# Product-key queries in one-pass products of split operands

## The chip, the cores and the metric

The kernel runs on one core of a Trainium2 chip. The metric is the device time of one execution in microseconds (us), the median of several executions. The engines are named as the profile names them: PE (TensorE matmuls), DVE (VectorE), ACT (ScalarE), POOL (GpSimd) and SP (SyncE, which issues most transfers).

## The reference, cut to what matters

One layer of a hybrid encoder trunk for 1024 prompt tokens and 64 sample tokens with 1024 channels. Its second half, which the change touches, is a retrieval of experts by product keys (PEER): for each token and each of 8 heads, a query with two halves of 128 channels, scores against 128 keys per half, the best 16 of each half, the best 16 of their sums, and then 16 experts out of 16384, each a row of a table `u` and a row of a table `v`.

```python
h = rmsnorm(x, norm2) * (1.0 + sc2) + sh2
x = x + g2 * peer(h, peer_wq, peer_keys, peer_u, peer_v)

def one_block(xb):                       # in peer, h in blocks of tokens
    q = (xb @ w_q).reshape(PEER_BLOCK, PEER_HEADS, 2, PEER_DQ // 2)
    s = jnp.einsum("nhcd,hckd->nhck", q, sub_keys).astype(jnp.float32)
    v1, i1 = lax.top_k(s[:, :, 0], PEER_TOPK)
    v2, i2 = lax.top_k(s[:, :, 1], PEER_TOPK)
    cand = (v1[..., :, None] + v2[..., None, :]).reshape(...)
    cidx = (i1[..., :, None] * PEER_NKEYS + i2[..., None, :]).reshape(...)
    top_s, pos = lax.top_k(cand, PEER_TOPK)
    eidx = jnp.take_along_axis(cidx, pos, axis=-1)
    gate = jax.nn.softmax(top_s, axis=-1)
    act = jax.nn.gelu(jnp.einsum("nd,nhkd->nhk", xb, u_tab[eidx]).astype(jnp.float32))
    coef = (gate * act).astype(xb.dtype)
    return jnp.einsum("nhk,nhkd->nd", coef, v_tab[eidx])
```

## The kernel before, in words

The five engines run programs of their own, written out by hand, and meet at semaphores. The order of each engine's program is the order of its work; nothing is planned at run time except a fixed assignment of PSUM banks (`plan`, `jobs`, `bank_for`) that says which engine empties which bank.

The first half of the layer ends with `mix` and the residual sum. DVE then normalizes the rows (`normed`, into `xn2`), PE transposes them (`turn("h2T", ...)`, 24 banks), and ACT and DVE turn each bank into columns of h2 by a scale and a bias (`modulated`, L329 and L332), taking alternate banks. h2 lies in `h2_buf` as float32, 8 blocks of 128 channels by 1088 tokens.

The head stage follows. For each of 8 heads PE runs six `query` groups (two halves c, three chunks of 384, 384 and 320 tokens), each of 8 float32 matmuls that accumulate over the 1024 channels (L904), and two `key_scores` groups of 9 matmuls (L919). The weights of a head, 128 x 2048, lie in one half of `wq_buf`, which SP loads two heads ahead; ACT copies the head's keys out of a block of all keys. Between every two query matmuls PE transposes half a tile of the u table (`turn_half`, four transposes of 128x128 into bank 6 or 7, L887), 14 tiles a head. ACT copies what PE made: a half tile back into one of 7 buffers (`table_half`, L1258), a query chunk (`q_move`, L1273), a group of scores (`s_moves`, L1286 and L1287, which waits until DVE has read the scores of the head before). SP stores each turned tile into `u_table` and loads the tile four later (`turn_table`). 128 tiles go this way; the rest is turned behind the last head.

DVE picks (`head_picks`): the top 16 of each half by maxima, index searches and replacements (L1868, L1873, L1875), the sums of the candidates (operations with two SBUF inputs), the top 16 of these sums, small integer operations, and a comparison with which it releases POOL (`positions_ready`). POOL decodes the indices of the head (`decode`, L584 to L601) while DVE goes on with the next one; DVE waits for the decode of the head before only ahead of its small operations. The softmax is shared: DVE subtracts the maximum, ACT takes the exponentials (`softmax_exp`, L1253 and L1254), and DVE sums them (L1951) and makes the gates. In ACT's program, the exponentials of head h-1 stand in the middle of head h, behind the copies of tile 10 and the last query chunk.

Behind the last head PE transposes the first 512 tokens of h2 back into rows (L952). Tokens from 512 on are needed later as a high part and a residual (`h_hi`, `h_lo`): ACT copies the high part, rounded, behind the last tile, and DVE subtracts (a rounded copy and the rest, which together hold the float32 value and let a product run as three products in one-pass format, `parts`). Then PE turns the picks, DVE and ACT make one-hots, PE the coefficients of the dense part, and POOL's gathers of table rows run beside the dense products until the end.

## Time and profile before

| what | before |
|---|---|
| three runs | 3021.05, 3023.61, 3029.80 us; median 3023.61 |
| profiled execution | 3024.45 us, span 3022.7 us, mean granted clock 0.97 |
| PE busy | 2822.1 us (93%) |
| PE weight loads | 2371.7 us (78%) |
| DVE busy | 2576.8 us (85%) |
| ACT busy | 911.7 us (30%) |
| POOL busy | 1579.1 us (52%) |

The busy times are sums over the whole span, and the stages differ. The page cuts the span in 40 slices of 75.6 us; the digits are tenths of busy time, and `PEclk` is the clock that TensorE was granted, in tenths of full speed. The head stage lies in slices 8 to 14.

```profile
PE   7999799999998577699999999999999999999996
PEld 3566358677776476699999999999999999999995
DVE  6481355369999999699999999999999999999998
ACT  3213230244444699312121121111211111112122
POOL 0000000025757000577777777777777777777772
PEclk9999899999999799899999999999999999999998
```

### The profile page before, as it was taken

To read this page: it belongs to the slowest core of one execution; us is meant where nothing else is said; L and a number is where in the kernel's file an instruction comes from. 1 tells how busy PE (TensorE), PEld (TensorE's weight loads), DVE (VectorE), ACT (ScalarE), POOL (GpSimd) and SP (SyncE) were. 2 spreads that over 40 slices of the span, in tenths; PEclk is the share of its full clock that TensorE was granted. 3 is DMA by queue.
4 is the path that set the end of the run, shared out by engine and by line. 5 is a ranking of instruction groups with operands and counts; after the bars stand their busy time and mean duration, and the time that the engine had idled before them with its cause. 6 is when DMAs were issued, how large, how long until landed. Compare 5 with 4: busy or idle time off the path is not lost.

```text
span 3022.7 us, 48458 instructions
## 1 busy us (share of the span) xinstructions
PE 2822.1 (93%) x16748; PEld 2371.7 (78%) x16748; DVE 2576.8 (85%) x5660; ACT 911.7 (30%) x1792; POOL 1579.1 (52%) x1211
## 2 busy tenths in 40 slices
PE   7999799999998577699999999999999999999996
PEld 3566358677776476699999999999999999999995
DVE  6481355369999999699999999999999999999998
ACT  3213230244444699312121121111211111112122
POOL 0000000025757000577777777777777777777772
PEclk9999899999999799899999999999999999999998
DMA  5012631499998566999999999999999999999996
GB/s 214 21 41 44 224 128 66 179 330 335 337 329 314 197 193 184 360 405 408 409 410 410 410 403 400 408 410 410 408 404 400 409 410 403 410 406 403 407 409 245
DMA packets 327375, 959.19 MB, mean 317 GB/s; under 512 B 38224, under 2 KB 119936, under 8 KB 313808
## 3 DMA queue, kind: packets, MB, share of 16 engines
q0 software_dynamic: 147456, 536.94, 44.8%
q1 hardware_dynamic: 167136, 412.46, 37.2%
q10 hardware_dynamic: 12688, 8.67, 1.0%
q8 instruction: 43, 0.70, 0.1%
q14 instruction: 52, 0.43, 0.0%
HBM read 840.97 MB, written 116.85 MB: 317 GB/s over the span
## 4 chain that ended last, share of the span: by engine, by line
PE 30%; DVE 26%; DMA 14%; issue 14%; POOL 11%; ACT 4%; DVEq 0%; ACTq 0%; SPq 0%; POOLq 0%
DMA ring<-in_vt,arena 12%; POOL ring L630 11%; PE ps L904 6%; DVE h_rows L2040 5%; DVE ring L2019 5%; PE ps L763 4%; PE ps L887 2%; PE ps L713 2%; PE ps L1010 2%; DVE u_lo L1479 2%; ACT arena L1342 2%; DVE y_rows L2040 2%; PE ps L861 2%; PE ps L870 2%; DVE arena L1479 2%
## 5 line engine op out<-in xcount | busy, mean ns | idle before, releaser
L630 POOL DMA_INDIRECT ring<-u_table,arena x512 | 690.3, 1348 | 375.4 <-PE ps L984 154.6
L630 POOL DMA_INDIRECT ring<-in_vt,arena x512 | 644.1, 1258 | 205.7 <-issue 134.8
L1010 PE MATMUL ps<-h_hi,u_hi 128*128 128x320 f32 (+1 forms) x2048 | 650.7, 318 | 35.1 <-DVE u_lo L1479 33.2
L2019 DVE SCALAR_TENSOR_TENSOR ring<-ring,h_rows 128x1024 f32<-128x1024 f32 x512 | 623.0, 1217 | 35.9 <-DMA ring<-u_table,arena 29.0
L1010 PE MATMUL ps<-h_lo,u_hi 128*128 128x320 f32 (+1 forms) x2048 | 607.4, 297 | 0.0
L1010 PE MATMUL ps<-h_hi,u_lo 128*128 128x320 f32 (+1 forms) x2048 | 607.3, 297 | 0.0
L1027 PE MATMUL ps<-w,v_rows 128*128 128x320 f32 (+1 forms) x2048 | 579.5, 405 | 0.0
L2040 DVE SCALAR_TENSOR_TENSOR h_rows<-ring,s5c,h_rows 128x1024 f32<-128x1024 f32 x381 | 489.7, 1285 | 41.9 <-DMA ring<-in_vt,arena 41.1
L1010 PEld LDWEIGHTS ps<-h_hi,u_hi 128*128 128x128 f32 x2048 | 389.5, 190 | 55.4 <-issue 25.3
L1027 PEld LDWEIGHTS ps<-w,v_rows 128*128 128x128 f32 x2048 | 358.3, 189 | 54.4
L1010 PEld LDWEIGHTS ps<-h_lo,u_hi 128*128 128x128 f32 x2048 | 389.5, 190 | 5.3
L1010 PEld LDWEIGHTS ps<-h_hi,u_lo 128*128 128x128 f32 x2048 | 389.2, 190 | 0.0
L1395 ACT ACTIVATE w<-ps 128x320 f32<-128x320 f32 (+1 forms) x256 | 104.7, 409 | 909.7 <-PE ps L1010 905.6
L1024 PE MATMUL ps<-w_hi,v_hi 128*128 128x320 f32 (+1 forms) x1024 | 366.0, 357 | 3.0 <-DVE y_sum L1479 3.0
L595 POOL TENSOR_TENSOR arena<-arena 128x2048 f32<-128x2048 f32 (+1 forms) x28 | 73.2, 2638 | 509.0 <-DVE arena L1479 508.5
L1479 DVE TENSOR_TENSOR arena<-arena 128x512 f32<-128x512 f32 (+17 forms) x229 | 187.0, 847 | 157.0 <-ACT arena L1175 62.9
L1024 PE MATMUL ps<-w_hi,v_lo 128*128 128x320 f32 (+1 forms) x1024 | 301.8, 295 | 0.0
L1024 PE MATMUL ps<-w_lo,v_hi 128*128 128x320 f32 (+1 forms) x1024 | 301.7, 295 | 0.0
L904 PE MATMUL ps<-h,wq 128*128 128x384 f32 (+1 forms) x768 | 266.9, 471 | 0.9 <-ACT h L329 0.9
L1024 PEld LDWEIGHTS ps<-w_hi,v_hi 128*128 128x128 f32 x1024 | 193.4, 189 | 24.6 <-DVE y_sum L1479 4.0
L1024 PEld LDWEIGHTS ps<-w_hi,v_lo 128*128 128x128 f32 x1024 | 193.4, 189 | 20.2
L984 PE MATMUL ps<-arena 128*128 128x128 f32 x1152 | 147.7, 285 | 54.8 <-DVE arena L2004 33.8
(279 smaller groups left out, 4337.4 us busy)
## 6 DMA issues: line engine op xcount, KB each, us to landing
u_turn<-in_ut SPq DMA_DIRECT2D x128, 512.0 KB, 5.3
u_table<-u_turn SPq DMA_DIRECT2D x128, 512.0 KB, 4.1
v_rows<-in_vt SPq DMA_DIRECT2D x64, 1024.0 KB, 11.0
u_raw<-in_ut SPq DMA_DIRECT2D x126, 512.0 KB, 6.7
coef_dram<-arena SPq DMA_DIRECT2D x8, 4096.0 KB, 15.9
c_raw<-coef_dram SPq DMA_DIRECT2D x64, 512.0 KB, 8.5
arena<-in_w_ada SPq DMA_DIRECT2D x24, 1024.0 KB, 7.5
arena<-in_xp SPq DMA_DIRECT2D x2, 4096.0 KB, 12.8
```

Source lines behind the costliest of these rows:

```text
L595: last = nc.gpsimd.tensor_tensor(v4, v4, itf[0:n, c, t0:t0 + nt, :].unsqueeze(2).to_broadcast(shp), ALU.mult)
L630: nc.gpsimd.indirect_dma_start(out=slot(n), out_offset=None, in_=table, in_offset=bass.IndirectOffsetOnAxis(ap=uvi[:, at:at + 1], axis=0)) ...
L763: last = mm(b[:, 0:width], w[:, k, P * m:P * m + P], h[:, k, P * k0:P * k0 + width], start=k == 0, stop=k == 7)
L904: last = mm(ps[q][:, 0:width], w[:, k, :], h2[:, k, P * k0:P * k0 + width], start=k == 0, stop=k == 7)
L984: last = mm(bank[:, j % 4, :], ar(PQ + 2048 * (g % 4) + P * j, P), ar(PQ + 2048 * (g % 4) + 1024 + P * j, P), start=True, stop=True)
L1010: last = mm(ps[b0 + j if first else j % 2][:, 0:width], w[a][:, k, :], ph[b][:, k, 64 * c0:64 * c0 + width], start=k == 0 and n == 0, stop ...
L1024: mm(out, v[r][:, P * d:P * d + P], w[r][:, 64 * c0:64 * c0 + width], start=begin and r % 2 == 0 and i == 0, stop=False, skip_group_check= ...
L1027: last = mm(out, v_row_buf(r)[:, 1024 + P * d:1024 + P * d + P], seg(w_in_buf, 1152 * r + ND + 64 * c0, width), start=False, stop=r % 2 == ...
L1395: av(seg(w_in_buf, o, width), ps[b0 + j if early and r < 2 else j % 2][:, 0:width], ACT.Gelu_apprx_tanh).then_inc(s("s_gelu"), 1)
L1479: return V.tensor_tensor(o, a, b, op)
L2019: V.scalar_tensor_tensor(out=row, in0=row, scalar=1.0, in1=h_rows[:, bass.ds(1024 * tile_of[0], 1024)], op0=ALU.mult, op1=ALU.mult, accum_ ...
L2040: V.scalar_tensor_tensor(out=y, in0=slot(at), scalar=acts[:, u, p:p + 1], in1=y, op0=ALU.mult, op1=ALU.add).then_inc(s("v_rows_done"), 1)
```

## The change

The queries are computed as the later dense products are: h2 is kept as a high part and a residual in the one-pass format (`s_hi`, `s_lo` for tokens 0 to 511, `h_hi`, `h_lo` for the others), the weights too, and each query group is three products per block of channels. The chunks are 512, 320 and 256 tokens. h2 is split before the first query: ACT or DVE computes each piece twice from its PSUM bank, once as float32 and once rounded, and DVE subtracts; the float32 buffer holds 512 tokens and is used twice. The last transposes, of 64 tokens, share one bank (17 banks for 24).

The weights of a head: ACT makes the high part (`wq_first`, two copies of 1024 columns a head, into one of two buffers), POOL the residual in the place of the weights (`wq_rest`, two subtractions, ahead of the decode of the head two earlier). PE's first query of each half waits for the residual. Keys come by two buffers, head by head, from SP.

The table has 6 buffers for 7 and 15 tiles a head for 14, 12 for 19 behind the last head. Head 0 has an order of its own on PE and ACT. The h2 rows are made by matmuls with a rounded identity from both parts. The split of h2 behind the last tile (ACT's copy and DVE's subtraction) is gone, and so are the waits for it.

The diff, cut to what the text speaks of:

```diff
-XN2, H2T = 0, 9216
-
-IALL, PICK, WQ, KEYS, QT, SB, WK = 17920, 21376, 27136, 31232, 33280, 35456, 37760
+XN2, HF, SHI, SLO, IDR = 33920, 43136, 9216, 13312, 51968
+
+IALL, PICK, WQ, KEYS, QT, SB, WK, WQH = 17408, 20864, 27136, 31232, 33280, 35456, (37760, 47232), (49792, 31232)
 CAND, CW2, D1, D0 = 38016, 40320, 42624, 44928
-TURN = (23296, 24320, 25344, 4608, 5632, 6656, 7680)
-NTURN, TPH = 7, 14
+TURN = (22784, 23808, 24832, 25856, 47744, 48768)
+NTURN, TPH = 6, 15
+QCH = ((0, 512), (512, 320), (832, 256))
+NSPLIT = 17
...
+            load(ar(WK[0], 256), A["keys"][:, 0:256], "wq_in0")
             load(seg(wq_buf, 0, 2048), A["wq"][0], "wq_in0")
             load(seg(wq_buf, 2048, 2048), A["wq"][1], "wq_in1")
             sp.wait_ge(bank_full, where["h2T", 7] + 1)
-            for r in range(3):
+            for r in range(4):
                 load(turn_buf[r][:, :], A["ut"][r], f"ut_in{r}")
-            stage_emptied(sp, "h2T")
-            load(turn_buf[3][:, :], A["ut"][3], "ut_in3")
+            sp.wait_ge(s("h_split"), NSPLIT)
+            load(ar(WK[1], 256), A["keys"][:, 256:512], "wq_in1")
...
-                    if not (first and r < 3):
-                        sp.wait_ge(s(f"table_out{b}"), 64 * i + 16 * ((r - 3) // NTURN) + 16)
+                    if not (first and r < NTURN - 4):
+                        sp.wait_ge(s(f"table_out{b}"), 80 * i + 16 * ((r + 4 - NTURN) // NTURN) + 16)
...
+                        load(ar(WK[h], 256), A["keys"][:, bass.ds(512 * i + (512 + 256 * h), 256)], f"wq_in{h}")
...
-            with pool.Fori(0, HEADS - 1) as h:
-                decode(h)
+            def wq_rest(h, hb):
+                for c in range(2):
+                    o = 2048 * hb + 1024 * c
+                    pool.wait_ge(s("wq_hi_ready"), 2 * h + c + 1)
+                    nc.gpsimd.tensor_tensor(wq_lo[:, o:o + 1024], seg(wq_buf, o, 1024),
+                                            wq_hi[hb][:, 1024 * c:1024 * c + 1024].bitcast(F32),
+                                            ALU.subtract).then_inc(s("wq_lo_ready"), 1)
+
+            wq_rest(0, 0)
+            wq_rest(1, 1)
+            with pool.Fori(0, HEADS // 2 - 1) as i:
+                for hb in range(2):
+                    wq_rest(2 * i + (hb + 2), hb)
+                    decode(2 * i + hb)
+            decode(HEADS - 2)
...
+            def query(hd, hb, c, q, of=0, tiles=(), first=False):
+
+                w = [v[:, o:o + 1024].rearrange("p (k n) -> p k n", k=8)
+                     for v, o in ((wq_hi[hb], 1024 * c), (wq_lo, 2048 * hb + 1024 * c))]
+                if q == 0:
+                    pe.wait_ge(s("wq_lo_ready"), 2 * hd + c + 1)
+                at, width = QCH[q]
+                c0 = (0, 0, 320)[q]
+                if first:
+                    h2_bank_emptied(q)
+                    pe.wait_ge(s("h_split"), (8, 16, NSPLIT)[q])
+                else:
                     pe.wait_ge(s("q_moved"), 3 * (2 * hd + c) + q - 2)
                 for k in range(8):
-                    last = mm(ps[q][:, 0:width], w[:, k, :], h2[:, k, P * k0:P * k0 + width],
-                              start=k == 0, stop=k == 7)
+                    for n, (a, b) in enumerate(parts):
+                        last = mm(ps[q][:, 0:width], w[a][:, k, :], parted[q > 0][b][:, k, c0:c0 + width],
+                                  start=k == 0 and n == 0, stop=k == 7 and n == 2)
                     if k == 7:
                         last.then_inc(s("q_full"), 1)
                     if tiles and k % 2:
-                        turn_half(of, tiles[k // 4], k // 2 % 2, first)
-
-            def key_scores(hd, c, first=False):
-                if c == 0:
-                    pe.wait_ge(s("kbuf_ready"), hd + 1)
+                        turn_half(of, tiles[k // 4], k // 2 % 2)
...
+            def head(hd, hb, i, last=False):
+                r0 = TPH * hb
+
+                query(hd, hb, 0, 1, i, (r0, r0 + 1))
+                query(hd, hb, 0, 2, i, (r0 + 2, r0 + 3))
+                query(hd, hb, 1, 0, i, (r0 + 4, r0 + 5))
+                turn_tile(i, r0 + 6)
+                key_scores(hd, hb, 0)
+                query(hd, hb, 1, 1, i, (r0 + 7, r0 + 8))
+                query(hd, hb, 1, 2, i, (r0 + 9, r0 + 10))
+                if not last:
+                    query(hd + 1, 1 - hb, 0, 0, i, (r0 + 11, r0 + 12))
+                    turn_tile(i, r0 + 13)
+                    turn_tile(i, r0 + 14)
+                key_scores(hd, hb, 1)
+
+            for q in range(3):
+                query(0, 0, 0, q, first=True)
+            stage_emptied(pe, "h2T")
+            turn_tile(0, 0, True)
+            key_scores(0, 0, 0, True)
+            for q in range(3):
+                query(0, 0, 1, q, 0, (2 * q + 1, 2 * q + 2))
+            turn_tile(0, 7)
+            key_scores(0, 0, 1)
+            query(1, 1, 0, 0, 0, (8, 9))
+            for r in range(10, TPH):
+                turn_tile(0, r)
             with pe.Fori(0, HEADS // 2 - 1) as i:
-                head(2 * i + 1, 1, i, i + 1)
-                head(2 * i + 2, 0, i + 1, i + 1)
-            head(HEADS - 1, 1, HEADS // 2 - 1, None)
+                head(2 * i + 1, 1, i)
+                head(2 * i + 2, 0, i + 1)
+            head(HEADS - 1, 1, HEADS // 2 - 1, last=True)
...
+            def h2_pieces(q, j, b, last):
+                g, n0, n = (0, 0, 512) if q < 2 else (1, 512, DSEQ)
+                v = b[:, 0:512] if q < 2 else b[:, 64 * j:64 * j + 64]
+                if q == 1:
+                    act.wait_ge(s("h_split"), j + 1)
+                for out in (h2[:, j, n0:n0 + n], h2_piece(0, q, j)):
+                    op = av(out, v, ACT.Identity, bias=mcol[:, 24 + j, g:g + 1], scale=a2[:, j, g:g + 1])
+                if last:
+                    done(op)
+
+            def wq_first(i, hb, c):
+                act.wait_ge(s(f"wq_in{hb}"), 32 * i + 32)
+                nc.scalar.copy(wq_hi[hb][:, 1024 * c:1024 * c + 1024], seg(wq_buf, 2048 * hb + 1024 * c, 1024)).then_inc(
+                    s("wq_hi_ready"), 1)
+
+            nc.scalar.copy(ident_r[:, :], ident[:, :])
+            for q in range(2):
+                for j in range(8):
+                    if j % 4:
+                        h2_pieces(q, j, filled(act, "h2T", 8 * q + j), True)
+                wq_first(0, 0, q)
+            b = filled(act, "h2T", 16)
+            for j in range(8):
+                h2_pieces(2, j, b, j == 7)
...
+                if first:
+                    for q in range(3):
+                        q_move(0, q)
+                    table_tile(0, 0)
+                    s_moves(0)
+                    stage_emptied(act, "h2T")
+                    act.wait_ge(s("h_split"), NSPLIT)
+                    wq_first(0, 1, 0)
+                    for q in range(3):
+                        moves(1, q, 2 * q + 1)
+                    wq_first(0, 1, 1)
+                    table_tile(0, 7)
+                    s_moves(1)
+                    for r in range(8, TPH):
+                        table_tile(0, r)
+                    return
...
                 q_move(0, 0)
                 moves(0, 1, 0)
                 moves(0, 2, 2)
                 moves(1, 0, 4)
-                table_tile(h, 6)
+                table_tile(i, r0 + 6)
                 s_moves(0)
+                if not last:
+                    wq_first(i + hb, 1 - hb, 0)
                 moves(1, 1, 7)
+                if not last:
+                    wq_first(i + hb, 1 - hb, 1)
                 moves(1, 2, 9)
-                if not first:
-                    softmax_exp(h - 1)
+                softmax_exp(h - 1)
                 if not last:
                     for r in range(11, TPH):
-                        table_tile(h, r)
+                        table_tile(i, r0 + r)
                 s_moves(1)
...
-            nc.scalar.copy(h_hi[:, :].rearrange("p (k n) -> p k n", k=8),
-                           seg(h2_buf, 0, 8704).rearrange("p (k n) -> p k n", k=8)[:, :, NSC:NT]).then_inc(
-                s("h_split"), 1)
...
+            def h2_pieces(q, j):
+                b = filled(dve, "h2T", 8 * q + j)
+                if q == 1:
+                    dve.wait_ge(s("h_split"), j + 1)
+                for out in (h2[:, j, 0:512], h2_piece(0, q, j)):
+                    last = ts(out, b[:, :], a2[:, j, 0:1], mcol[:, 24 + j, 0:1], ALU.mult, ALU.add)
+                done(last)
+
+            for q in range(2):
+                for j in range(8):
+                    if j in (0, 2):
+                        h2_pieces(q, 2 * j)
+                    stage_emptied(dve, "h2T", 8 * q + j + 1)
+                    tt(h2_piece(1, q, j), h2[:, j, 0:512], h2_piece(0, q, j).bitcast(F32), ALU.subtract).then_inc(
+                        s("h_split"), 1)
             stage_emptied(dve, "h2T")
+            tt(parted[1][1][:, :, 512:ND], h2[:, :, 512:ND], parted[1][0][:, :, 512:ND].bitcast(F32),
+               ALU.subtract).then_inc(s("h_split"), 1)
...
-            dve.wait_ge(s("h_split"), 1)
-            for b in range(3, NTURN):
-                table_stored(dve, b)
-            tt(h_lo[:, :].rearrange("p (k n) -> p k n", k=8),
-               seg(h2_buf, 0, 8704).rearrange("p (k n) -> p k n", k=8)[:, :, NSC:NT],
-               h_hi[:, :].rearrange("p (k n) -> p k n", k=8).bitcast(F32), ALU.subtract).then_inc(s("h_split"), 1)
-            dve.wait_ge(s("h_split"), 2)
```

## Rows read from the trace of the kernel before

**Rows 1.** Windows: us; busy us per engine (instructions); TensorE clock; DMA share; GB/s.
```profile
811.00:860.00 49.00, 48.52 (x256) 34.70 (x255) 46.96 (x264) 23.59 (x45) 33.50 (x26) 1.00 0.93 334
963.00:1000.00 37.00, 25.12 (x115) 20.08 (x116) 36.32 (x213) 16.13 (x28) 21.59 (x15) 0.62 1.02 417
```

**Rows 2.** DVE timeline, where heads begin: start us, us, line, tiles [idle before].
```profile
605.64 0.06 DVE L1865 MEMSET arena<- 128x1 f32 x1 [30.86 <-ACT arena L1287]
629.09 0.29 DVE L1868 MAX8 arena<-arena 128x8 f32<-128x128 f32 x1 [12.34 <-issue]
...
665.50 0.36 DVE L1951 TENSOR_REDUCE arena<-arena 128x8 f32<-128x128 f32 x2 [8.07 <-ACT arena L1254]
667.50 0.29 DVE L1868 MAX8 arena<-arena 128x8 f32<-128x128 f32 x1 [0.27 <-DVE arena L1479]
...
811.40 0.06 DVE L1865 MEMSET arena<- 128x1 f32 x1 [0.57 <-DVE arena L1479]
...
859.91 0.29 DVE L1868 MAX8 arena<-arena 128x8 f32<-128x128 f32 x1 [0.56 <-DVE arena L1479]
```

**Rows 3.** DVE waits, 600 to 1015 us: total us, times, longest.
```profile
DVE arena L1951 <- ACT arena L1254: 17.5, 4, 8.1
```

**Rows 4.** DVE timeline: two-input operations without and beside POOL work.
```profile
640.12 0.69 DVE L1479 TENSOR_TENSOR arena<-arena 128x512 f32<-128x512 f32 x1
640.73 0.80 DVE L1479 TENSOR_TENSOR arena<-arena 128x384 f32<-128x384 f32 x3
...
854.85 4.50 DVE L1479 TENSOR_TENSOR arena<-arena 128x128 f32 x2 [0.15 <-DVE arena L1955]
...
882.12 2.30 DVE L1479 TENSOR_TENSOR arena<-arena 128x512 f32<-128x512 f32 x1
884.34 2.25 DVE L1479 TENSOR_TENSOR arena<-arena 128x384 f32<-128x384 f32 x3
```

**Rows 5.** POOL timeline: start and end of one decode; residuals of a u tile.
```profile
854.06 5.25 POOL L595 TENSOR_TENSOR arena<-arena 128x2048 f32<-128x2048 f32 x2 [14.41 <-DVE arena L1479]
...
887.59 0.57 POOL L601 TENSOR_TENSOR arena<-arena 128x128 f32 x2 [0.18 <-POOL arena L601]
...
1053.60 5.71 POOL L616 TENSOR_TENSOR u_lo<-u_raw,u_hi 128x1024 fp32r<-128x1024 f32 x2 [68.43 <-ACT u_hi L1334]
```

**Rows 6.** PE timeline: queries (x4 are two matmuls), transposes, key scores.
```profile
629.55 1.46 PE L904 MATMUL ps<-h,wq 128*128 128x384 f32 x4
630.84 0.60 PE L887 MATMUL ps<-ident,u_turn 128*128 128x128 f32 x4
631.28 1.46 PE L904 MATMUL ps<-h,wq 128*128 128x384 f32 x4
...
649.05 2.31 PE L919 MATMUL ps<-arena 128*128 128x128 f32 x18
```

**Rows 7.** PE timeline: one-pass matmuls, 512 and 320 columns.
```profile
500.20 0.39 PE L870 MATMUL ps<-w_hi,ys_hi 128*128 128x512 f32 x1
500.44 0.40 PE L870 MATMUL ps<-w_lo,ys_hi 128*128 128x512 f32 x1
...
1505.53 0.31 PE L1010 MATMUL ps<-h_hi,u_lo 128*128 128x320 f32 x1
1505.68 0.31 PE L1010 MATMUL ps<-h_hi,u_hi 128*128 128x320 f32 x1
```

**Rows 8.** ACT timeline: h2 before the queries.
```profile
561.93 2.76 ACT L329 ACTIVATE h<-ps,mcol,a 128x512 f32<-128x512 f32 x4
...
573.40 1.96 ACT L329 ACTIVATE h<-ps,mcol,a 128x512 f32<-128x512 f32 x5 [0.51 <-PE ps L697]
```

**Rows 9.** Windows of PE alone: the transposes behind 5.2 us of rest.
```profile
566.70:570.00 3.30, 3.28 (x16) 0.50 0.93 315
```

**Rows 10.** ACT and DVE timeline behind the last head.
```profile
1017.33 0.70 ACT L1323 COPY arena<-ps 128x512 f32<-128x512 f32 x2 [0.64 <-PE ps L967]
...
1017.14 4.95 DVE L1479 TENSOR_TENSOR h_lo<-h,h_hi 128x4608 fp32r<-128x4608 f32 x1
```

More of the change, by code:

```diff
@@ L137, in trunk @@
         h_hi, h_lo = rounded("h_hi", HHI, 4608), rounded("h_lo", HLO, 4608)
+        s_hi, s_lo = rounded("s_hi", SHI, 4096), rounded("s_lo", SLO, 4096)
+        wq_hi = [rounded(f"wq_hi{b}", WQH[b], 2048) for b in range(2)]
+        wq_lo = rounded("wq_lo", WQ, 4096)
+        ident_r = rounded("ident_r", IDR, P)
         u_hi, u_lo = rounded("u_hi", UH, 2048), rounded("u_lo", UR, 2048)
@@ L268, in trunk @@
         jobs("mix", 36, "dve")
-        jobs("h2T", 24, lambda i: "act" if i % 2 else "dve")
+        jobs("h2T", 17, lambda i: "dve" if i % 4 == 0 and i < 16 else "act")
         n_stage = {}
@@ L333, in modulated, with h2_piece @@
                                                 ALU.mult, ALU.add).then_inc(emptied["dve"], 1)
+        parted = [[v[:, :].rearrange("p (k n) -> p k n", k=8) for v in pair] for pair in ((s_hi, s_lo), (h_hi, h_lo))]
+        h2 = seg(h2_buf, 0, 4608).rearrange("p (k n) -> p k n", k=8)
+        def h2_piece(part, q, j):
+            return parted[q > 0][part][:, j, :] if q == 0 else parted[1][part][:, j, 512 * (q - 1):ND if q > 1 else 512]
         @block.sync
@@ L426, in _ @@
             sp.wait_ge(s("xn2_ready"), NTILE)
-            load(ar(KEYS, 2048), A["keys"], "keys_in")
+            load(ar(WK[0], 256), A["keys"][:, 0:256], "wq_in0")
             load(seg(wq_buf, 0, 2048), A["wq"][0], "wq_in0")
@@ L475, in _ @@
             sp.wait_ge(s("indices_ready"), 1)
-            sp.wait_ge(s("h_split"), 2)
+            sp.wait_ge(s("h_split"), NSPLIT)
             for e in range(2):
                 load(seg(u_in_buf, 1024 * e, 1024), A["ut"][e], f"ut_in{e}")
-            table_stored(sp, 0)
+            for b in range(NTURN):
+                table_stored(sp, b)
             for e in range(2):
@@ L872, in _, with h2_bank_emptied, turn_half @@
                     full(last)
-            turn("h2T", 8, lambda t, j: ar(xn2_at(t) + P * j, P), lambda j: ar(xn2_at(8) + P * j, P, DSEQ),
-                 "xn2_ready")
-            stage_emptied(pe, "h2T")
-            h2 = seg(h2_buf, 0, 8704).rearrange("p (k n) -> p k n", k=8)
-            pe.wait_ge(s("keys_in"), 16)
-            def turn_half(hd, r, half, first=False):
+            for q in range(2):
+                pe.wait_ge(s("xn2_ready"), 4 * q + 4)
+                for j in range(8):
+                    b = bank_for(pe, "h2T", 8 * q + j)
+                    for t in range(4):
+                        last = nc.tensor.transpose(b[:, P * t:P * t + P], ar(xn2_at(4 * q + t) + P * j, P), ident[:, :])
+                    full(last)
+            pe.wait_ge(s("xn2_ready"), NTILE)
+            b = bank_for(pe, "h2T", 16)
+            for j in range(8):
+                last = nc.tensor.transpose(b[:, 64 * j:64 * j + 64], ar(xn2_at(8) + P * j, P, DSEQ),
+                                           ident[0:DSEQ, 0:DSEQ])
+            full(last)
+            stage_emptied(pe, "mix")
+            def h2_bank_emptied(b):
+                stage_emptied(pe, "h2T", max(i + 1 for i in range(17) if where["h2T", i] % 8 == b))
+            parts = ((0, 0), (0, 1), (1, 0))
+            def turn_half(i, r, half, first=False):
                 if half == 0:
-                    pe.wait_ge(s(f"ut_in{r % NTURN}"), 32 * hd + 16 * (r // NTURN) + 16)
+                    pe.wait_ge(s(f"ut_in{r % NTURN}"), 80 * i + 16 * (r // NTURN) + 16)
                 if not (first and r == 0):
-                    pe.wait_ge(s("ut_moved"), 2 * TPH * hd + 2 * r + half - 1)
+                    pe.wait_ge(s("ut_moved"), 4 * TPH * i + 2 * r + half - 1)
                 for k in range(4):
@@ L937, in _ @@
-            kbuf = ar(WK, 256).rearrange("p (c n) -> p c n", c=2)
-            query(0, 0, 0, 0, 0, first=True)
-            head(0, 0, 0, 0, True)
+            def head(hd, hb, i, last=False):
[12 more added lines that the diff above has]
+                key_scores(hd, hb, 1)
@@ L951, in _ @@
                     for k in range(4):
-                        last = nc.tensor.transpose(ps[2 * t + half][:, P * k:P * k + P],
-                                                   h2[:, 4 * half + k, P * t:P * t + P], ident[:, :])
+                        for n in range(2):
+                            last = mm(ps[2 * t + half][:, P * k:P * k + P],
+                                      parted[0][n][:, 4 * half + k, P * t:P * t + P], ident_r[:, :],
+                                      start=n == 0, stop=n == 1)
                     last.then_inc(s("rows_full"), 1)
             pe.wait_ge(s("h_rows_ready"), 2 * NS)
-            for r in range(TPH * HEADS - 3, P):
+            for r in range(TPH * HEADS - 4, P):
                 turn_tile(0, r)
@@ L1968, in _ @@
             assert got == NLINK, got
-            table_stored(dve, 2)
+            for b in (2, 3):
+                table_stored(dve, b)
             i1, i2 = ar(IALL, NSC), ar(IALL + 1152, NSC)
```

74 lines of the change are left out of this document (27 added, 47 removed).

## The prediction

> **What bounds the kernel now.** I read the slices of the page first, then the windows, then the timeline of each engine through the stage that the change touches: queries, key scores, top-16 and the turning of the u table, from 575 to 1022 us. In a late head PE is busy for 48.5 of 49 us and DVE for 47.0 [rows 1]. Two engines look like the bound, so the view that decides is the idle time ahead of DVE, which picks the top 16 and whose last pick everything later waits for. Head 0 begins on DVE at 605.64, stands 12.34 us for its second scores and 8.07 us for the softmax exponentials, which ACT issues only between two queries of the next head. Head 1 begins at 667.50, head 4 at 811.40, head 5 at 859.91 [rows 2]. The exponentials hold DVE up four times, for 17.5 us, the longest being head 0's 8.1 [rows 3]. From head 4 on, no such wait is left: DVE takes 48.51 us a head, and PE is already ahead.
>
> Why 48.51? Head 0's two candidate sums, with POOL at rest, take 0.69 and 0.80 us; in a late head they take 2.30 and 2.25, and the gate product takes 4.50 and ends at 859.35 [rows 4], 0.04 us behind the end of POOL's first pair of the decode, 854.06 + 5.25 = 859.31 [rows 5]. So DVE's operations with two SBUF inputs stand while POOL works on one. Heads 1 to 3 last 811.40 - 667.50 = 143.9 us together, against 3 x 48.51 = 145.5: where DVE waited for the exponentials, it met less of the decode, so those waits cost nearly nothing net. This decides the sum.
>
> The Trainium skill (SBUF — State Buffer, "SBUF: two separate sides") says that DVE and GpSimd share one port pair as an exclusive lock, which the loser waits out for a whole instruction; by that rule, the trace agrees. It also speaks against this change, which gives POOL more to do: the second rival.
>
> **The change part by part.**
>
> *Queries.* Two of them with 384 columns take 1.29 us (629.55 to 630.84), 0.645 each; 320 columns I scale to 0.54 [rows 6]. One head half now costs 16 x 0.645 + 8 x 0.54 = 14.6 us. One-pass matmuls follow each other every 0.24 us at 512 columns and 0.15 at 320 [rows 7]; 256 I put at 0.12. The new half is 24 x (0.24 + 0.15 + 0.12) = 12.2 us. Saved: 2.4 a half, 4.8 a head, 38 us in all, on PE.
>
> *Fifteen table tiles a head for fourteen.* Half a tile is four transposes, 0.44 us (630.84 to 631.28), a tile 0.88. By its parts PE's head is now 29.2 + 28 x 0.44 + 2 x 2.24 for two key scores (2.31 busy, 2.24 to the next query [rows 6]) = 46.0 us, and then 24.4 + 13.2 + 4.5 = 42.1. DVE still needs 48.51. From head 1 on PE's gain is worth nothing: ACT will stand at the exponentials, some 5 us a head, and PE behind it.
>
> *Splitting h2, before the queries.* Now the first query starts when ACT's last five pieces end, 573.40 + 1.96 = 575.4 [rows 8]. Afterwards ACT makes 12 of 16 large pieces, each twice. From 561.93, at 2.76 / 4 = 0.69 each, the first half ends at 570.5. A weight copy of 1024 columns follows (at most 1.4, twice a 512) and may wait for its load, which has landed by 575.4: I take 573. Then 8.3 for the second half, a weight copy, and 16 small pieces at about 0.32 (of the 1.96, 0.69 was a large one): 588. DVE's residuals, some 0.7 each, run beside and end about a microsecond later; they are covered, since DVE is idle for 30.86 us there [rows 2]. The third product ends at 592. PE's first product starts near 577 on a slow clock: behind 5.2 us of rest the granted clock was 0.50, the 1.2 GHz level [rows 9]. That costs at most 24 x 0.24 = 5.8 us, which the wait for the last split hides.
>
> *Where head 1 then begins on DVE.* Up to head 0's exponentials PE still has three key scores (2.24 us each), 26 tiles (22.9), three query halves (36.6), and about 3.5 us of turns between copies where tiles stand alone: 592 + 6.7 + 22.9 + 36.6 + 3.5 = 662. Before, the exponentials ended at 665.5. So a gain of 3 us is left of two cheaper heads; the rest went into the later start. DVE's first scores come near 597 (592, a tile, key scores, a copy of 1.5) and its second near 618, by the same list, and not at 629, but that only lengthens the wait for the exponentials.
>
> *POOL's residuals of the weights.* They are two operations a head of the kind that splits a u tile, 5.71 / 2 = 2.86 us each [rows 5]. The pair for head h+2 is ahead of head h's decode in POOL's order, and behind ACT's copy of the second high part, one query ahead of the exponentials. For head 0: 662 - 4.7 + 1.4 + 2.9 = 661.6. There decode 0 begins. DVE's gate product stands until its first pair is done, and the next head follows 859.91 - 854.06 = 5.85 us behind the decode's start: 667.5, the old time. I take 668. In later heads the decode is 34.1 us long (854.06 to 888.16, from 42.7 us into a head, to 28.3 into the next); the residuals take 28.3 to 34.0. The candidate sums are over at 26.7 (886.6 less 859.9), and then come the maxima and index searches. I price them at nothing; the other end is 5.7 us a head. PE's first query of head h+1 newly waits for them; behind it in PE's order stand four tiles and the second key scores of head h. Those are due 11 us into head h on DVE, 25 us after the residuals end, so nobody is late.
>
> *DMA.* A head moves 15 x 2 x 0.524 + 1.05 + 0.13 = 16.9 MB. The remainder of the table ran at 417 GB/s, 1.02 of the engines; a head ran at 334, with 0.93 [rows 1]. At 417 a head needs 40.5 us, at 334 / 0.93 = 359 it needs 47.1. Both are below 48.51. Six buffers for seven leave two stores between a buffer's store and its reload. I cost this at nothing; the cover is DVE's head. The keys come in 0.13 MB pieces, and ACT no longer copies them: about nothing. The rows of h2, in twice as many matmuls, run behind the last head, where PE has time.
>
> *Behind the last head.* The h2 split, 4.95 us on DVE from 1017.14 to 1022.09, is gone. Late next are the turned picks: ACT's last copy ends at 1017.33 + 0.70 = 1018.03 [rows 10]. The one-hots, and with them the coefficients and the gathers, start 4.1 us sooner after the picks. Remaining tiles, 12 for 19, are done long before.
>
> *The sum.* Head 1 at 668 (+0.5); heads 1 to 3 at 48.51 each bring head 4 to 813.5 (+2.1); heads 4 to 7 are unchanged; then -4.1. Together -2.0 us. The profiled execution took 3024.45 us; 3022.5 after. The median shown is 0.84 below it: 3021.6, forecast 3022.
>
> **The rivals.**
>
> *The start is worth more.* If ACT reaches head 0's exponentials early, head 1 begins early. Its floor is a DVE that never waits: first scores near 597, a head 0 of 667.5 - 605.6 - 12.3 - 8.1 = 41.5 us, head 1 at 638.5, 29 us sooner; with -4 and +1.6, about 2992. For it: 20.4 us of waits in head 0. Against: the program puts the exponentials behind eleven tiles of head 1, and the PE list above leaves 3 us. I expect no more than half: 3007. Akin to it: the weight residuals push the decode past the gate product, which saves up to 4.5 us in each of six heads, 27 us: 2995. It needs PE's loop to be about as slow as DVE's.
>
> *Slower: POOL takes the port at a bad time.* Place: the small two-input operations from 37 us into a head. Price: 2.86 us for one residual, 5.7 for two, in six heads: 17 to 34 us, so 3039 to 3056. It decides when ACT's copy of the second high part comes later than 34 us into DVE's head. By my count it comes near 31, so 3 us separate the two. Against it: top-16 searches showed no lengthening beside the decode. By the lock that the Trainium skill states, a residual that starts just ahead of a sum or a gate product costs its full length, and one beside the searches nothing.
>
> *Slower: the table paces the loop.* If a head can only move 334 GB/s, its 16.9 MB take 50.6 us; 2.1 us more in six heads and a first head some 8 us later make +21 - 4: 3041. For it: 0.93 of the engines were taken now. Against it: 417 GB/s in the remainder, same transfers.
>
> *The change doesn't do what it says:* the pitch of 0.24 and 0.15 us was read where no transposes stand between the products; if they stretch, so that a half costs 14.6 us as before, the three halves put the exponentials 7 us later: 3029, within the forecast's range.
>
> **How the numbers follow.** A measurement of this kernel can tell about 0.3%, 9.1 us: faster is under 3014.5, slower above 3032.7. The forecast's mechanism (DVE keeps the pace) holds 0.54, 3015 to 3032; the two faster cases 0.25 together; port and table 0.13 and 0.08. From these: faster 0.25, same 0.54, slower 0.21. The range of 8 in 10 reaches half into the faster cases and to the table's price: 3003 to 3041.
>
> **What would show it.** Right: heads 4 to 7 on DVE still 48.5 us apart, candidate sums still 2.3 us, idle PE and ACT in each head, head 1 on DVE between 664 and 672, one-hots about 1 us after the indices, queries in groups of 24 at 0.24, 0.15 and 0.12 us. Wrong: DVE heads of 46 us or less with a gate product below 1 us; DVE idle before its scores in late heads; POOL's residuals at 37 us into a head with longer small operations there; a table pace above 3.2 us a tile.

## The result, and the profile after

The changed kernel takes 3090.39 us (median of 4 runs, 3088.17 to 3093.09), the kernel before 3024.3 (3021.05 to 3029.8, 4 runs beside it): a ratio of 1.0214, 95% interval 1.0201 to 1.0227. It is 66 us slower. The forecast was 3022 us, its range ended at 3041, and none of its rivals names what happened. The profiled execution took 3093.09 us, its span is 3091.3.

Start where the prediction started, with the stretches of [rows 1] in the changed kernel: us, then busy us (instructions) of PE, PEld, DVE, ACT and POOL, the granted TensorE clock, DMA share, GB/s.

```profile
811.00:860.00 49.00, 39.19 (x256) 34.14 (x255) 37.94 (x212) 20.97 (x39) 30.31 (x20) 0.90 0.81 300
963.00:1000.00 37.00, 24.34 (x168) 22.61 (x167) 36.08 (x233) 12.75 (x26) 15.46 (x13) 0.82 0.62 224
```

No engine is near its limit any more in a late head: PE fell from 48.52 to 39.19 us, DVE from 46.96 to 37.94, the DMA share from 0.93 to 0.81. So the loss is a wait. DVE's waits from 560 to 1100 us, which answer to [rows 3] (total us, times, longest):

```profile
DVE arena L1977 <- issue: 31.4, 6, 9.6
DVE arena L1974 <- issue: 29.3, 5, 6.7
DVE arena L2060 <- ACT arena L1332: 24.6, 1, 24.6
```

The third line is head 0's exponentials, 8.07 us before. The first two are new. "Issue" means that the engine waited for nothing that the profile shows. DVE's timeline at one head's begin, with ACT's copies of the scores in the next fence (start us, us, instruction, [idle before <- what ended it]):

```profile
832.46 4.68 DVE L1571 TENSOR_TENSOR arena<-arena 128x128 f32 x2 [0.15 <-DVE arena L2064]
842.81 0.06 DVE L1974 MEMSET arena<- 128x1 f32 x1 [5.67 <-issue]
842.81 0.87 DVE L1977 MAX8 arena<-arena 128x8 f32<-128x128 f32 x4
848.23 1.06 DVE L1977 MAX8 arena<-arena 128x8 f32<-128x128 f32 x5 [4.55 <-issue]
```

```profile
837.18 1.08 ACT L1362 COPY arena<-ps 128x512 f32<-128x512 f32 x2 [1.56 <-PE ps L965]
838.14 0.26 ACT L1363 COPY arena<-ps 64x128 f32<-64x128 f32 x1
```

The gate product ends at 837.14. These copies are the head's second scores (the first were copied earlier), so at 838.40 all data is there; DVE begins at 842.81. Then it stops again between the fourth and the fifth of nine equal MAX8, where no semaphore stands. The pair of stops comes in all five heads that DVE reaches by a jump back in its loop over heads 1 to 6: 5.59 to 6.66 us at the begin and 4.08 to 4.76 behind the fourth MAX8, 51.0 us together (the 9.6 us in the first line is another thing, head 0's second scores). The head went from 48.51 us [rows 2] to 56.

Two more such pairs stand in the gather stage, 118 us apart, at the first operation (L1571 on `w`) and the next (the gate weights, L1571 on `s5c`) of one of its four DVE loops, the one for the third tile of tokens, which jumps back twice. They are all of DVE's "issue" stops above 1.5 us there, 17.2 us:

```profile
2365.72 0.49 DVE L1571 TENSOR_TENSOR w<-w,c_raw 128x320 f32<-128x320 f32 x1 [4.18 <-issue]
2370.53 0.17 DVE L1571 TENSOR_TENSOR s5c<-s5c,gates 128x8 f32<-128x8 f32 x1 [4.32 <-issue]
...
2483.75 0.49 DVE L1571 TENSOR_TENSOR w<-w,c_raw 128x320 f32<-128x320 f32 x1 [4.37 <-issue]
2488.56 0.17 DVE L1571 TENSOR_TENSOR s5c<-s5c,gates 128x8 f32<-128x8 f32 x1 [4.32 <-issue]
```

And one line of the page's table of DMA queues (packets, MB, share of the engines) changed without any reason in the data (the other queue of instructions, q8, moved 43 packets before and 45 after). First the kernel before, then after:

```profile
q14 instruction: 52, 0.43, 0.0%
```

```profile
q14 instruction: 88, 0.72, 0.1%
```

This queue, which loads instructions, moved 36 packets more, of 0.72 MB / 88 = 8.2 KB each. That gives the theory.

**Theory A, code loading.** DVE's program comes to it over q14, in pieces of 8.2 KB (that the queue is DVE's is so far a guess; the edits below, which touch DVE alone, test it too). DVE's loop over heads 1 to 6 is 289 instructions long in the built program (waits, registers and branches counted), the gather loop 263. If a loop lies over too many pieces, a jump back finds its first pieces gone and waits for them. The change made no loop longer. It made the program ahead of the heads' loop 31 instructions longer, by the split of h2 on DVE, and moved the loop from places 795 to 1083 to places 826 to 1114. The stop behind the fourth MAX8 puts an edge between pieces at place 832. The second stop of the third gather loop (3004 to 3266 after, 2977 to 3239 before) falls at place 3007 or 3008, and 832 + 17 x 128 = 3008: edges every 128 places fit both. Further edges are then 960, 1088 and so on. By these both loops lay over three pieces before and lie over four now, the first with 27 instructions from place 1088 on, the second with 3 from 3264 on. DVE's four other loops lie over three pieces in both kernels (one has 288 instructions, three have 263), and none shows such a stop. The Trainium skill (Vector Engine (DVE) Microarchitecture Reference, "1.2 Instruction fetch and dispatch (NX sequencer)") states 64 bytes an instruction; by that 128 of them are 8.2 KB, and the packets agree.

**Rivals.** B: the scores come late from PE and ACT. C: POOL's subtractions of the weights hold DVE's port. D: the table's transfers pace the heads. E and G: instructions added to DVE's program cost in themselves, wherever its loops lie.

### The profile page after: what moved, and what is told of

It is laid out like the page before. It is cut to its first block, busy times and chain, and to the rows that moved or that the text cites. A ratio compares the mean times of both kernels' runs of the same rounds, so it can differ in the third digit from the quotient of the medians.

```text
span 3091.3 us, 49415 instructions
## 1 busy us (share of the span) xinstructions
PE 2808.8 (91%) x17164; PEld 2428.6 (79%) x17164; DVE 2587.2 (84%) x5672; ACT 930.6 (30%) x1825; POOL 1606.5 (52%) x1227
## 4 chain that ended last, share of the span: by engine, by line
DVE 30%; PE 25%; issue 17%; DMA 13%; POOL 9%; ACT 4%; DVEq 0%; ACTq 0%; SPq 0%; POOLq 0%
DMA ring<-in_vt,arena 10%; POOL ring L658 9%; DVE h_rows L2143 5%; DVE ring L2122 4%; PE ps L791 4%; PE ps L1067 3%; DVE arena L1982 3%; DVE arena L1977 2%; PE ps L1084 2%; DVE arena L1571 2%; PE ps L741 2%; DVE y_rows L2143 2%; PE ps L1081 2%; ACT arena L1434 2%; DVE u_lo L1571 2%
## 5 line engine op out<-in xcount | busy, mean ns | idle before, releaser
L658 POOL DMA_INDIRECT ring<-u_table,arena x512 | 672.6, 1314 | 400.3 <-PE ps L1042 158.2
L658 POOL DMA_INDIRECT ring<-in_vt,arena x512 | 652.9, 1275 | 213.9 <-issue 130.2
L1571 DVE TENSOR_TENSOR arena<-arena 128x512 f32<-128x512 f32 (+17 forms) x229 | 189.5, 858 | 155.9 <-ACT arena L1231 62.9
L628 POOL TENSOR_TENSOR wq_lo<-wq,wq_hi 128x1024 fp32r<-128x1024 f32 x16 | 39.4, 2471 | 422.6 <-ACT wq_hi L1315 421.2
L928 PE MATMUL ps<-ident,u_turn 128*128 128x128 f32 x1024 | 163.2, 292 | 62.2 <-ACT u_turn L1336 36.5
L928 PEld LDWEIGHTS ps<-ident,u_turn 128*128 128x128 f32 x1024 | 129.4, 150 | 85.5 <-ACT u_turn L1336 44.8
```

Of the source, the lines that this page charges most:

```text
L658: nc.gpsimd.indirect_dma_start(out=slot(n), out_offset=None, in_=table, in_offset=bass.IndirectOffsetOnAxis(ap=uvi[:, at:at + 1], axis=0)) ...
L928: last = nc.tensor.transpose(ps[6 + half][:, P * k:P * k + P], seg(turn_buf[r % NTURN], 512 * half + P * k, P), ident[:, :])
L1571: return V.tensor_tensor(o, a, b, op)
```

## Experiments: where the loop lies

Five kernels move the loops and do nothing else, by N memsets of one column each on DVE, ahead of head 0 (0.06 us each; the first takes over a wait, so the loops move by N - 1). The edit, with 16, 4, 8, 30 or 44 for N:

```diff
+            for j in range(N):
+                V.memset(small["itf"][:, j:j + 1], 0.0)
             head_picks(0, True)
```

**N = 16 on the changed kernel.** 

> The changed kernel with 16 one-column memsets more on DVE ahead of head 0's search (each about 0.06 us, where DVE waits for the first scores anyway); nothing else differs. They move DVE's loop over heads 1 to 6 some 15 places down its program. Theory A (code loading): the changed kernel's DVE stood 5.7 to 6.7 us at the start of each head of the loop but the first and 4.1 to 4.8 us after the fourth MAX8 (29.3 and 21.8 us in the trace) and twice 4.2 + 4.3 us at the start of one of the gather loops (17.1 us), because each of these two loops, 289 and 263 instructions, lay over four loaded pieces of code (88 packets of 8.2 KB on q14 against 52); moved down by 15, each lies over three. A expects the issue waits gone, q14 back to about 50 packets, and 3090 - 68 = 3022 us (3015 to 3030). Rival B (the scores come late from PE and ACT), rival C (POOL's subtractions of the weights hold DVE's port), rival D (the table's DMAs pace the heads): nothing of theirs is touched, 3090 us.

**N = 4 on the kernel before.** 

> The kernel before with 4 such memsets ahead of head 0's search: a control. Theory A: the loop of 289 instructions is moved 3 places down and still lies over three pieces of code (its last instruction is 2 places ahead of the end of the third, by the place where the changed kernel's DVE stalled): 3024 us, no issue waits. Rivals B to D: 3024 us as well. A rival E, that any instruction added to DVE's stream costs, has 0.2 us.

**N = 8 on the kernel before.** 

> The kernel before with 8 such memsets, 4 more than the control: nothing of the change is in it. Theory A: the loop's last three instructions now lie in a fourth piece; every jump back (five) finds its first piece gone, so each head but the first of the loop stands about 5.7 us at its start; the piece ends 29 instructions into the loop, some 6 us of work, in which the next piece may arrive, so the second stall of 4.4 us may be hidden. 3024 + 29 to 3024 + 51, 3053 to 3075 us, all of it in the heads; the gather loops stay as they were. Rivals B to D: 3024 us.

**N = 30 on the kernel before.** 

> The kernel before with 30 such memsets, which puts both loops at about the places that they have in the changed kernel (3 places higher in the heads' loop, 1 lower in the gather loop). Theory A: the whole loss without any part of the change, 51 us in the heads and 17 in the third gather loop, 3024 + 68 = 3092 us (3080 to 3097), with stalls at the start of each head and after about the seventh MAX8. Rivals B to D: 3024 us.

**N = 44 on the kernel before.** 

> The kernel before with 44 memsets ahead of head 0's search: 14 more than the run that lost 47 us. Theory A (a loop is only slow where its place makes it lie over a fourth piece of code): the heads' loop now begins 6 places behind the edge at which the changed kernel stalled, and lies over three pieces again; so does the third gather loop: 3026 us plus the memsets' 1 to 2 us, no issue waits, 53 packets or so on q14. Rival G (more instructions on DVE's program mean more loading): 3073 us or more.

Measured (ratio to the kernel before on the same chip, 95% interval; pieces by the edges above):

| kernel | heads' loop | pieces | third gather loop | pieces | q14 packets | median us | ratio |
|---|---|---|---|---|---|---|---|
| before | 795-1083 | 3 | 2977-3239 | 3 | 52 | 3024.3 | |
| before, N = 4 | 798-1086 | 3 | 2980-3242 | 3 | 52 | 3028.35 | 1.0008 (0.9999-1.0017) |
| before, N = 8 | 802-1090 | 4 | 2984-3246 | 3 | 77 | 3040.92 | 1.0053 (1.0037-1.0068) |
| before, N = 30 | 824-1112 | 4 | 3006-3268 | 4 | 87 | 3072.97 | 1.0158 (1.0142-1.0173) |
| before, N = 44 | 838-1126 | 3 | 3020-3282 | 3 | 53 | 3028.8 | 1.0003 (0.9993-1.0012) |
| after | 826-1114 | 4 | 3004-3266 | 4 | 88 | 3090.39 | 1.0214 (1.0201-1.0227) |
| after, N = 16 | 841-1129 | 3 | 3019-3281 | 3 | 53 | 3039.22 | 1.0043 (1.0029-1.0057) |

Theory A holds in every row as to which loop stops and which does not, and the rivals fall: by B, C and D the memsets would have changed nothing, and E and G are answered by N = 4 and N = 44. Four memsets more (N = 4 to 8) cost the kernel before 13 us, with nothing of the change in it; fourteen more (30 to 44) take 44 us away again (47 by the ratios). It is the number of pieces that decides, and not how near the first edge is: with N = 8 the gather loop begins 24 places ahead of an edge and does not stop, while the longer heads' loop begins 30 places ahead of one and does. The packets count the jumps: 25 more than 52 for 5 jumps back with N = 8, 35 for 7 with N = 30, and 35 between the changed kernel with and without its memsets, again for 7; five packets a jump. With N = 8 the edge lies 30 places into the loop, and DVE's timeline shows the second stop there, 4.0 us behind the loop's begin (0.9 in the changed kernel) and short, since the piece was on its way meanwhile; the third line below is the stop:

```profile
823.26 0.06 DVE L1865 MEMSET arena<- 128x1 f32 x1 [5.76 <-issue]
823.26 1.83 DVE L1868 MAX8 arena<-arena 128x8 f32<-128x128 f32 x9
...
828.53 0.29 DVE L1873 FIND_INDEX8 arena<-arena 128x8 uint32<-128x128 f32 x1 [1.23 <-issue]
```

With N = 30 it lies 8 places in, and DVE's timeline shows it behind the sixth MAX8, two later than in the changed kernel, whose loop begins two places further on; in the gather loop the two stops have become one of 8 us, as only that loop's first two instructions, which compute registers, lie ahead of the edge:

```profile
771.67 0.06 DVE L1865 MEMSET arena<- 128x1 f32 x1 [3.43 <-issue]
771.67 1.26 DVE L1868 MAX8 arena<-arena 128x8 f32<-128x128 f32 x6
777.17 0.67 DVE L1868 MAX8 arena<-arena 128x8 f32<-128x128 f32 x3 [4.25 <-issue]
...
2347.36 0.49 DVE L1479 TENSOR_TENSOR w<-w,c_raw 128x320 f32<-128x320 f32 x1 [8.27 <-issue]
```

The sizes were overestimated three times: 13 to 15 us where 29 to 51 were expected, 47 where 68, 51 of the 68 in the changed kernel. The stops alone sum to 29 us with N = 8, 56 with N = 30 and 68 in the changed kernel; but while DVE stood, other waits got shorter. In the kernel before DVE stands for exponentials in the early heads, 17.7 us in all with N = 4 but 13.2 with N = 8. In the changed kernel a stopped DVE met less of POOL's work: its candidate sums took 1.81 and 0.80 us (813.35 and 815.08), while 2.46 and about 2.3 are usual without the stops. These two examples make up a part of the difference; the rest was not followed up.

## Experiments: what the change is worth without the stops

The changed kernel with N = 16 is still 0.43% slower than the kernel before (0.29 to 0.57), some 13 us, though the forecast for just this case was a gain of 2. Its DVE timeline, at the begins of head 1 and head 4, at a gate product and at the first one-hots:

```profile
668.37 0.35 DVE L2060 TENSOR_REDUCE arena<-arena 128x8 f32<-128x128 f32 x2 [25.40 <-ACT arena L1332]
669.02 3.16 DVE L1571 TENSOR_TENSOR arena<-arena 128x128 f32<-128x128 f32 x2
672.45 0.06 DVE L1974 MEMSET arena<- 128x1 f32 x1 [0.27 <-DVE arena L1571]
...
815.29 4.69 DVE L1571 TENSOR_TENSOR arena<-arena 128x128 f32 x2 [0.15 <-DVE arena L2064]
820.52 0.30 DVE L1977 MAX8 arena<-arena 128x8 f32<-128x128 f32 x1 [0.54 <-DVE arena L1571]
...
869.21 0.06 DVE L1974 MEMSET arena<- 128x1 f32 x1 [0.54 <-DVE arena L1571]
...
1027.72 1.22 DVE L1571 TENSOR_TENSOR arena<-iota,arena 128x1024 f32<-128x1024 f32 x1 [0.91 <-ACT arena L1416]
```

A head is 869.21 - 820.52 = 48.69 us, with a gate product of 4.69. ACT now waits for DVE at the exponentials:

```profile
ACT arena L1331 <- DVE arena L1571: 36.3, 6, 8.9
```

**Gate product first.** Theory A2: what paces these heads is DVE, held up by POOL's decode at the gate product; PE's gain lies idle behind it. The edit moves sum, reciprocal and gate product ahead of the one-hots of the positions, which release POOL's decode (shortened; the remarks behind # are not in the code):

```diff
+                if not last_head:
+                    gate_products()   # wait for the exponentials; sum, reciprocal, gate product
                 for n, t0, nt in ((P, 0, 8), (DSEQ, 8, 1)):
                     shp = [n, nt, TOPK, TOPK]
                     last = tt(ar(D0 + 256 * t0, 256 * nt, n)...
...
-                dve.wait_ge(s("softmax_exp"), h + 1)   # and the same, for all heads
+                if last_head:
+                    gate_products()
```

> The changed kernel with 16 memsets as above (no loading stalls) and one more edit: in every head but the last, DVE makes the softmax's sum, reciprocal and gate product ahead of the one-hots of the positions, whose end starts POOL's decode, and not behind them. Theory A2 (without the loading stalls the heads are paced by DVE, whose gate product stands 4.7 us behind POOL's first decode operation while PE and ACT wait some 6 us a head at the exponentials): the gate product falls to about 0.6 us, heads go from 48.70 us to about 45, the pace at which PE and ACT went from head 0's exponentials to head 1's (667.93 to 712.87, 44.9 us), six heads: 3039 - 22 = 3017 us (3013 to 3022). Rival F (PE, ACT or the table's DMAs already pace those heads and DVE's wait is only where their slack shows): 3039 us, with DVE waiting for scores. Rival C (POOL's subtractions of the weights cost DVE): heads stay above 47 us.

Measured: 3016.58 us, 0.9969 of the kernel before (0.9955 to 0.9984). DVE's timeline has the gate product at 0.37 us, and the lock that it left has moved to the second candidate sum, 5.69 us for 2.28:

```profile
833.70 5.69 DVE L1571 TENSOR_TENSOR arena<-arena 128x384 f32<-128x384 f32 x3
...
854.22 0.37 DVE L1571 TENSOR_TENSOR arena<-arena 128x128 f32 x2 [0.15 <-DVE arena L2018]
```

Heads are 46.0 us on average (reciprocals at 669.39 and, six heads later, 945.17) where 45 were expected, and the dense one-hots come at 1011.23, 16.5 us sooner than with N = 16. So 16.5 of the 22.6 us between the medians stand in the heads; the rest was not found. In the stretch of [rows 1] PE, DVE and the DMAs are now all near their limit, PE at 46.20 of 49 us, DVE at 47.90, the DMAs at 0.99:

```profile
811.00:860.00 49.00, 46.20 (x327) 41.24 (x328) 47.90 (x281) 27.50 (x51) 40.72 (x28) 1.00 0.99 364
```

**The same edit on the kernel before** (with N = 2, which leaves its loops where they don't stop). 

> The same edit on the kernel before (2 memsets, so that the loop stays where it does not stall). A2 with the prediction's account of PE (46 to 47 us a head before the change): heads 1 to 5 were already 47.15 us apart with DVE waiting for exponentials, the two late ones at 48.3 and 48.5, so only some 3 us are to be had: 3023 to 3026 us. Rival F: 3026 us. A rival in which DVE's own work paced the kernel before in all heads: 3026 - 20 = 3006 us.

Measured: 3024.89 us, ratio 0.9995 (0.9986 to 1.0004). Heads are 47.15 us throughout, and DVE waits for exponentials in every one, here in its list of waits:

```profile
DVE arena L1905 <- ACT arena L1254: 21.8, 7, 10.8
```

PE is busy for 247.5 of the 250 us from 700 to 950 there. So before the change PE paced the heads as soon as DVE was quicker, and the edit bought nothing. The two belong together: the change takes PE out of the way, the edit takes POOL out of DVE's way.

**Head 0's exponentials earlier**, with the gate product first and without. ACT's heads 1 and 2 are written out ahead of its loop, and in head 1:

```diff
                 q_move(0, 0)
                 moves(0, 1, 0)
+                if early:
+                    softmax_exp(h - 1)
...
-                softmax_exp(h - 1)
+                if not early:
+                    softmax_exp(h - 1)
```

> As the changed kernel with memsets and the gate product first, and ACT makes head 0's exponentials behind the second query copy of head 1 (about 638 us, when DVE's maxima are there) and not behind the fifth (668 us); for this ACT's heads 1 and 2 are written out ahead of its loop. Theory A2 with the prediction's first rival (the start is worth more): DVE's head 1 begins when its scores come, about 660 us, and not at 672; later heads go at the 44.9 us of PE and ACT, so that the scores of head 7 come at about 927 and no longer at 941: some 12 us off e5, 3005 us (3000 to 3012), and faster than the kernel before by 0.5 to 0.9 %. Rival F: as e5 or slower.

> The exponentials of head 0 early as in the run before, without the gate product's edit: DVE's head 1 begins near 662 and not at 672.5, heads of 48.7 us follow: 3039 - 10 = 3029 us (3024 to 3034). Rival F: 3039 us.

Measured: 3017.51 us with the gate product first (0.9974, 0.9964 to 0.9984), the same as without this edit; 3034.14 alone (1.0028, 1.0018 to 1.0037), 5 us below N = 16 (1.0043); but these two intervals overlap, and the one-hots of its trace come at 1029.84, 2.1 us later than with N = 16, so a gain is not shown. The expected 12 and 10 us did not come. In the first of them DVE's head 1 begins 14.6 us earlier and then stands at its second scores, which PE makes hardly sooner (ACT copies them from 678.93 on, without this edit from 680.12):

```profile
657.91 0.29 DVE L1982 MAX8 arena<-arena 128x8 f32<-128x128 f32 x1 [12.80 <-issue]
...
680.19 0.29 DVE L1982 MAX8 arena<-arena 128x8 f32<-128x128 f32 x1 [11.17 <-issue]
```

## Why the prediction was wrong, by its steps

- *"DVE still needs 48.51."* This step failed, and with it the forecast. It took a head's length from the work that a head does. DVE's instructions are as long as before, but the loop's code no longer stayed loaded, at 10 us a jump. Taking only the stops away returned 51 of the 66 us. The split of h2 was costed by the time of its instructions, "covered, since DVE is idle"; that they also take places in the program, ahead of a loop with 4 places to spare, was nowhere in the sum. The trace of before could not price it, but DVE's program and the packets of q14 stood there to be weighed. The Trainium skill (Runtime: NRT & Kernel Launch, "Instruction fetch mechanics") says that a taken branch whose target is outside the current window forces a load before work goes on: the rule that spoke against this change, and the prediction weighed another one. The runs agree with the rule, but not with its window of two blocks of 256 instructions: the stop at place 3008 asks for pieces of 128, and loops over three of these do not stop.
- *Without the stops, DVE keeps the pace, and PE's gain is worth nothing.* Right in kind: 48.69 us a head, a gate product of 4.69 us, ACT waiting 36.3 us in six heads, where "some 5 us a head" was said.
- *Head 1 on DVE at 668, exponentials at 662.* Mis-sized. With N = 16 the first scores came at 593.79 (597 was said), but the exponentials at 667.93 and head 1 at 672.45. PE's list allowed 0.88 us a tile; the last half of tile 9 and tiles 10 to 14 of head 0 took from 620.25 to 631.75, 11.5 us for 4.8, as PE's timeline shows:

```profile
620.25 1.04 PE L928 MATMUL ps<-ident,u_turn 128*128 128x128 f32 x8
621.53 3.32 PE L928 MATMUL ps<-ident,u_turn 128*128 128x128 f32 x20 [0.24 <-ACT u_turn L1336]
627.45 1.97 PE L928 MATMUL ps<-ident,u_turn 128*128 128x128 f32 x8 [2.60 <-DMA u_turn<-in_ut]
630.13 1.97 PE L928 MATMUL ps<-ident,u_turn 128*128 128x128 f32 x8 [0.71 <-DMA u_turn<-in_ut]
```

  They wait 3.3 us for the table's loads, in a stretch (600 to 632 us) where the DMAs are at 0.95 and 352 GB/s, and they are slower behind the waits, 1.97 us for eight transposes and not 1.04: the granted clock was 1.00 from 620 to 624 us and 0.50, the 1.2 GHz level, from 628 to 632. The DMA step was costed at nothing, "the cover is DVE's head"; head 0 has no such cover.
- *Heads 1 to 3 at 48.51.* 148.1 us for 145.5. Head 1 took 50.77, the next two 48.66 and 48.64. Most of the 2.1 us more is one copy behind the top-16 search of the sums, which lasts until POOL's residual ends (709.39 + 2.39 = 711.78); in DVE's other heads both copies of this line together take 0.22 us. From POOL's and DVE's timelines:

```profile
709.39 2.39 POOL L628 TENSOR_TENSOR wq_lo<-wq,wq_hi 128x1024 fp32r<-128x1024 f32 x1 [2.34 <-ACT wq_hi L1315]
```

```profile
709.90 1.90 DVE L2004 COPY arena<-arena 128x8 f32<-128x8 f32 x1
```

- *POOL's residuals cost nothing.* Right in all heads but head 1: in head 3 of N = 16 they run as a pair of 4.72 us at 800.47, 28.6 us into the head, beside the index searches, and POOL then waits 9.5 us for DVE. In head 1 the second one came late, 37 us into the head, as POOL had waited 2.34 us for ACT's copy, and it cost 1.7 us by DVE's copy above. So the port rival did occur at its place, but in one head and not in six, and at 1.7 us where 2.86 was the price. With the gate product first the same copies take 0.58 to 0.97 us in five heads. They have one SBUF input, so the prediction's rule, which names operations with two, is too narrow.
- *The table rival* did not occur in the changed kernel (0.81 and 300 GB/s). With the gate product first it is close: the DMA share is 0.99 in a late head, and PE waits for the table's loads, 22.0 us from 560 to 1040 us and 8.3 of them from 690 to 960. PE's head of 42.1 us, by the prediction's list, came in no run; the shortest average over six heads was 46.0. PE's waits with the gate product first:

```profile
PE ps L928 <- DMA u_turn<-in_ut: 22.0, 16, 3.2
```

- *New query pitch.* Right: 0.23, 0.15 and 0.12 us; the fourth rival fell.
- *Behind the last head, -4.1 us.* Right: from the conversion of the indices (1023.67) to the one-hots 4.05 us, before it was 8.04 (1014.09 to 1022.13).
- *The start is worth more.* Its price, 15 to 29 us, fell with the two last kernels: the second scores come at PE's pace, and PE in turn waits for the table (19.6 us from 560 to 1040, with the DMAs at 0.99 from 640 to 700). *Decode past the gate product*, 2995, was the right mechanism for a further edit: made on purpose it gave 22.6 us of the 27, 16.5 of them in the heads, as the second candidate sum took part of it back.

By the terms above the one-hots began 5.6 us later with N = 16 than in the profile before, where -2.0 was forecast. In these two profiles the gather stage, which the change does not touch, was another 4.8 us longer. From the first one-hots to DVE's last instruction it took 1996.6 to 1999.4 us in four profiles of the kernel before (those without stops) and 1997.5 to 2005.8 in the four of the changed kernel with 16 memsets, so among the latter it varies by 8 us. Of the 13 us between the medians this part, some 5 to 8 us, stays open.

## What to carry to other kernels

Before pricing an edit by its instructions, look at the loops behind it: where a trace has "issue" stops at a loop's first instruction and again a little further on, and the queue of instructions moves more packets than it did before the change (52 to 55 here in the runs without stops, 77 to 88 in those with them), the loop's place is likely the cost, and some idle instructions ahead of it move it. Test that first, since until it is repaired no other part of a change can be read from the time. Then ask again which engine paces: here the change, rid of the stops, lost 0.4%, the reordering of the gate product alone was worth nothing, and the two together gained 0.3%.

## What the hardware showed that was not expected

A jump back in DVE's loop showed no stop while the loop lay over three pieces of code. When three instructions or more lay in a fourth, DVE stopped for 3.4 to 6.7 us at the loop's begin and up to 4.8 us at the first edge inside it, or once for 8.3 to 8.7 us where that edge came right behind the begin; five packets of 8.2 KB were loaded at each such jump. The second stop shrinks with the work between the loop's begin and the edge: 4.4 us behind one memset and four MAX8, 1.2 or less behind 4.0 us of work. The same was seen in two loops of 289 and 263 instructions. Loops of other engines were not tried.

A DVE copy with a single SBUF input, of 128x8, took 1.90 us beside a subtraction of POOL and ended with it; the pair of such copies takes 0.22 us elsewhere.
